# Block products of gate and up kept as running sums in PSUM, in a two-layer encoder on one core

## The chip, the cores and the metric

The kernel runs on one NeuronCore of a Trainium2 chip. The metric is the device time of one launch in microseconds (us). The kernel before was timed three times: 1349.25, 1349.61 and 1349.74 us, median 1349.61. One further execution was taken with the hardware profiler. Engines are named as in the profile: PE is TensorE, PEld its weight loads, DVE is VectorE, ACT is ScalarE, POOL is GpSimd, SP issues the DMAs.

## The reference

```python
# D_MODEL 1024, SEQ 512, FFN_HIDDEN 2816, two layers
def swiglu(x, w_gate, w_up, w_down):
    return (jax.nn.silu(x @ w_gate) * (x @ w_up)) @ w_down

for layer in range(2):
    h = attn_conv_mixer(...) if layer == 0 else retention_mixer(...)
    x = layer_norm(alpha * x + h, ln_mix_g, ln_mix_b)
    x = layer_norm(alpha * x + swiglu(x, w_gate, w_up, w_down), ln_ffn_g, ln_ffn_b)
```

Layer 0 mixes with grouped-query attention beside a depthwise convolution, layer 1 with a retention scan in two directions. Both end in the SwiGLU above, and only its two products `x @ w_gate` and `x @ w_up` (512 by 1024 by 2816 each, float32) are touched here.

## The kernel before, in words

Every float32 operand of a product is split into a high and a low part (float32r), and a product takes three matmuls: high by high, high by low, low by high (`product`, L1878 to L1882). ACT makes the high part by a copy, DVE the low part by a subtraction.

The hidden width of 2816 is 22 tiles of 128 rows (`NH`). Weights come in chunks of 1 MB, each with two hidden tiles of `w_gate` or of `w_up`: chunk `c_ffn + 2i` is the gate of pair i, `c_ffn + 2i + 1` the up of pair i. Two buffers (`raw`, `w_hi`, `w_lo`) alternate, and `load` (L408) fetches a chunk when the split of the chunk two before it in the same buffer is done. The first three chunks (`PLAIN`) are multiplied plainly. The other 19 in each layer (`FAST`) are multiplied as 2 by 2 blocks with seven block products in place of eight, in Winograd's form of Strassen's scheme. These are the block chunks. The first block chunk is the up of pair 1 (`third` in the code), the second the gate of pair 2 (`fourth`), the third the up of pair 2. The second and third are `fast_pair(2)`, pairs 3 to 9 are a loop, pair 10 is the last.

A block product (`fast_product`, L2253) is 4 steps of 3 matmuls of 128 by 128 by 256, so 12 matmuls, and a block chunk is 84. The blocks of the weights are partly sums: DVE makes three of them (`weight_sums`, L1544 to L1546), POOL a fourth in place in `raw` (`fourth_sum`, L707). ACT and DVE then split in two pieces: piece 0 is the three sums (`sum_hi`, `sum_lo`, 128x1536), piece 1 the whole chunk (`w_hi`, `w_lo`, 128x2048); `piece_hi` is L983, `piece_lo` L1550. The sums of the token side (`mix_hi`, `mix_lo`, and one block of `xT` that is replaced, `mix_split(3)` and `mix_lo_part(3)`) are made once in each layer.

PSUM has eight banks. A gate chunk uses the four of `SIDE_A`, an up chunk those of `SIDE_B`. Before the change PE writes the seven products of a block chunk in this order: a11 b11, s2 t2, s1 t1, a12 b21, s4 b22, s3 t3, a22 t4. ACT copies the first into `gate32` or `up32` (`product_copy`, L993), and PE waits for that copy ahead of the sixth product, which goes into the same bank. DVE makes the four output blocks with five additions (L1566, L1572, L1574, L1576, L1578), the last three after the chunk's last product or close to it. When both chunks of a pair are summed, ACT applies Silu to the gate (`fast_gate`, L998) and DVE multiplies it by up (`fast_up`, L1584).

What sets the order of the work is the order in which each engine's instructions are written, since every engine takes its own in that order, and semaphores between engines: `product_made`, `product_copied`, `tile_added`, `sums_made`, `piece_hi_made`, `lo_made`, `gate_made`, `h_made`. A block chunk may start on PE when its `w_lo` is made (`lo_made`) and when the additions of the chunk two before it, which used the same banks, are done (`tile_added`).

Of the kernel before, what the change touches and what calls it, by code (L numbers as in the profile page):

```python
# [98 lines left out]
ADDS = 5  # L99
# [3 lines left out]
def build_encoder(nc, ins, out):  # L103
    ctx = ExitStack()
    with ctx:
# [645 lines left out]
        def _(act):  # L751
# [204 lines left out]
            def swiglu(layer, c_ffn, c_down, pm):  # L956
# [32 lines left out]
                def product_copy(i, up, n):  # L989

                    act.wait_ge(product_made, 3 * n + 1)
# [16 lines left out]
                def fast_pair(i, last=False):  # L1008
# [3 lines left out]
                    product_copy(i, 0, n)  # L1012
                    piece_hi(up, n + 1, 1)
                    if last:
                        product_copy(i, 1, n + 1)
                        make_hi(act, Chunk(c_down))
                        rows_hi(0)
                        fast_gate(i, n)
                    else:
                        piece_hi(later, n + 2, 0)  # L1020
                        product_copy(i, 1, n + 1)
                        piece_hi(later, n + 2, 1)
                        fast_gate(i, n)
# [13 lines left out]
                act.sem_inc(hi_made, 1)  # L1037
                mix_split(3)
                piece_hi(Chunk(c_ffn + 4), fourth, 0)
                product_copy(1, 1, third)  # L1040
# [182 lines left out]
        def _(dve):  # L1223
# [300 lines left out]
            def swiglu(layer, c_ffn, c_down, pm):  # L1524
# [10 lines left out]
                def weight_sums(ch, n, first=False):  # L1535
# [3 lines left out]
                    dve.wait_ge(raw_landed[ch.s], 16 * ch.nth + 16)  # L1539
                    if first:  # L1540
                        dve.wait_ge(x_normed, 8 * (2 * layer + 1))
                    else:
                        dve.wait_ge(lo_made, ch.lo - 1)
                    mine(nc.vector.tensor_tensor(w_sum[:, 0], a21, a22, ALU.add), wait=False)  # L1544
                    mine(nc.vector.tensor_tensor(w_sum[:, 2], a11, a21, ALU.subtract))
                    nc.vector.tensor_tensor(w_sum[:, 1], w_sum[:, 0], a11, ALU.subtract).then_inc(sums_made, 1)  # L1546
# [15 lines left out]
                def first_add(up, n):  # L1562
                    dst, (a, b, c, d) = (gate32, up32)[up], BANKS_OF[up]
                    dve.wait_ge(product_made, 3 * n + 2)
                    dve.wait_ge(product_copied, n + 1)
# [954 lines left out]
```

## Time and profile before

| | |
|---|---|
| median of three runs | 1349.61 us |
| profiled execution, its own time | 1349.3 us |
| span of its instructions | 1347.5 us |
| PE busy (7880 matmuls) | 1329.9 us, 99% of the span |
| PEld busy | 1180.2 us, 88% |
| DVE busy | 970.3 us, 72% |
| ACT busy | 575.6 us, 43% |
| POOL busy | 144.5 us, 11% |
| DMA queue q1, share of 16 engines | 29.6% |

Busy time of PE is the union of its matmuls, whose ends are modelled and which overlap; how fast PE goes is read from the distance between two starts. The profiled execution's own time is 1.8 us longer than its span. The two SwiGLU stages are alike: the block chunks run from 264.04 to 455.5 us in layer 0 and 762.5 us later in layer 1.

### The profile page before, as it was taken

The numbers are of one execution on the slowest core, as the hardware profiler recorded it, in microseconds if no ns is written. First come the engines' busy times: TensorE is split into PE (matmuls) and PEld (weight loads), VectorE is DVE, ScalarE is ACT, GpSimd is POOL, SyncE is SP. The second block draws the span as 40 slices with busy tenths as digits, with TensorE's granted clock in tenths as the row PEclk, the third lists the DMA queues.
The fourth block names the chain that finished last, engine by engine and source line by source line (L and its number), as shares of the span: only waits on it lengthen the run. The fifth ranks groups of instructions, "written<-read, shape, count | busy, mean of one in ns | idle before, by whom it ended". The sixth has DMA issues, their size and how long they took to land.

```text
span 1347.5 us, 19504 instructions
## 1 busy us (share of the span) xinstructions
PE 1329.9 (99%) x7880; PEld 1180.2 (88%) x7880; DVE 970.3 (72%) x1215; ACT 575.6 (43%) x735; POOL 144.5 (11%) x141
## 2 busy tenths in 40 slices
PE   9999999999999999999999999999999999999997
PEld 8887888999999988898888888878899999998885
DVE  5999957898888533477877778763389988874336
ACT  3468834534434322345354544543154443442221
POOL 5011013111111000030000000000040111100001
PEclk9999999999999999999999999999999999999999
DMA  6210113333233323251123140324323422333321
GB/s 227 63 63 1 32 63 95 94 96 123 93 96 122 125 96 103 83 204 63 63 94 125 63 156 32 125 75 171 98 63 94 125 94 93 125 125 99 107 77 63
DMA packets 86352, 131.74 MB, mean 98 GB/s; under 512 B 2832, under 2 KB 61456, under 8 KB 86160
## 3 DMA queue, kind: packets, MB, share of 16 engines
q1 hardware_dynamic: 86288, 130.84, 29.6%
q8 instruction: 46, 0.75, 0.2%
q14 instruction: 18, 0.15, 0.0%
HBM read 126.63 MB, written 4.19 MB: 97 GB/s over the span
## 4 chain that ended last, share of the span: by engine, by line
PE 87%; DVE 8%; ACT 2%; POOL 1%; issue 1%; DMA 0%; SPq 0%; DVEq 0%; ACTq 0%
PE ps L1880 22%; PE ps L1882 21%; PE ps L1881 21%; PE ps L1958 19%; DVE acc L1264 2%; DVE w_lo L426 2%; ACT w_hi L422 1%; POOL w_lo L426 1%; PE ps L2135 1%; PE ps L1893 1%; DMA x_tok<-in_x 0%; PE ps L2322 0%; PE ps L2090 0%; PE ps L2089 0%; DVE x_tok L1504 0%
## 5 line engine op out<-in xcount | busy, mean ns | idle before, releaser
L1880 PE MATMUL ps<-xT_hi,w_hi 128*128 128x256 f32 (+1 forms) x992 | 302.2, 305 | 0.5 <-POOL w_lo L426 0.5
L1882 PE MATMUL ps<-xT_hi,w_lo 128*128 128x256 f32 (+1 forms) x992 | 301.1, 304 | 0.0
L1881 PE MATMUL ps<-xT_lo,w_hi 128*128 128x256 f32 (+1 forms) x992 | 301.1, 303 | 0.0
L426 DVE TENSOR_TENSOR w_lo<-raw,w_hi 128x2048 fp32r<-128x2048 f32 x44 | 100.9, 2292 | 185.7 <-ACT w_hi L422 185.6
L1880 PEld LDWEIGHTS ps<-xT_hi,w_hi 128*128 128x128 f32 x992 | 189.5, 191 | 8.8 <-POOL w_lo L426 1.1
L1882 PEld LDWEIGHTS ps<-xT_hi,w_lo 128*128 128x128 f32 x992 | 189.5, 191 | 7.6
L1881 PEld LDWEIGHTS ps<-xT_lo,w_hi 128*128 128x128 f32 x992 | 189.6, 191 | 7.3
L422 ACT ACTIVATE w_hi<-raw 128x2048 fp32r<-128x2048 f32 x50 | 95.7, 1915 | 210.1 <-PE ps L1958 151.7
L983 ACT ACTIVATE sum_hi<-w_sum 128x1536 fp32r<-128x1536 f32 x38 | 56.5, 1488 | 183.4 <-PE ps L1882 182.6
L1880 PE MATMUL ps<-mix_hi,sum_hi 128*128 128x256 f32 x456 | 129.0, 283 | 0.0
L1881 PE MATMUL ps<-mix_lo,sum_hi 128*128 128x256 f32 x456 | 129.0, 283 | 0.0
L1882 PE MATMUL ps<-mix_hi,sum_lo 128*128 128x256 f32 x456 | 129.0, 283 | 0.0
L1958 PE MATMUL ps<-w_hi,h_hi 128*128 128x512 f32 x352 | 109.0, 390 | 0.4 <-DVE h_lo L1588 0.4
L1958 PE MATMUL ps<-w_lo,h_hi 128*128 128x512 f32 x352 | 108.8, 389 | 0.0
L1958 PE MATMUL ps<-w_hi,h_lo 128*128 128x512 f32 x352 | 108.8, 389 | 0.0
L1550 DVE TENSOR_TENSOR w_lo<-raw,w_hi 128x2048 fp32r<-128x2048 f32 x38 | 87.1, 2292 | 17.5 <-ACT w_hi L983 17.3
L707 POOL TENSOR_TENSOR raw<-raw,w_sum 128x512 f32<-128x512 f32 x38 | 51.1, 1344 | 346.1 <-DVE w_sum L1546 346.1
L1880 PEld LDWEIGHTS ps<-mix_hi,sum_hi 128*128 128x128 f32 x456 | 87.6, 192 | 0.0
L1881 PEld LDWEIGHTS ps<-mix_lo,sum_hi 128*128 128x128 f32 x456 | 87.6, 192 | 0.0
L1882 PEld LDWEIGHTS ps<-mix_hi,sum_lo 128*128 128x128 f32 x456 | 87.6, 192 | 0.0
L1099 ACT ACTIVATE w_hi<-raw 128x1024 fp32r<-128x1024 f32 x54 | 56.0, 1055 | 72.6 <-PE ps L1882 56.4
L1958 PEld LDWEIGHTS ps<-w_hi,h_hi 128*128 128x128 f32 x352 | 65.6, 188 | 14.4 <-issue 1.1
(249 smaller groups left out, 2727.4 us busy)
## 6 DMA issues: line engine op xcount, KB each, us to landing
raw<-in_l_w_in SPq DMA_DIRECT2D x33, 1024.0 KB, 5.2
raw<-in_l_ffn_w_gate SPq DMA_DIRECT2D x22, 1024.0 KB, 5.3
raw<-in_l_ffn_w_up SPq DMA_DIRECT2D x22, 1024.0 KB, 5.2
raw<-in_l_ffn_w_down SPq DMA_DIRECT2D x22, 1024.0 KB, 4.9
raw<-in_l_w_out SPq DMA_DIRECT2D x12, 1024.0 KB, 5.1
x_tok<-in_x SPq DMA_DIRECT2D x4, 512.0 KB, 6.9
x_kept<-x_tok SPq DMA_DIRECT2D x1, 2048.0 KB, 11.6
x_tok<-x_kept SPq DMA_DIRECT2D x4, 512.0 KB, 8.1
```

What stands on the lines that cost most here:

```text
L422: act.activation(w_hi[ch.s][:], raw[ch.s][:], ACT.Copy).then_inc(hi_made, 1)
L426: eng.tensor_tensor(w_lo[ch.s][:], raw[ch.s][:], f32(w_hi[ch.s][:]), ALU.subtract)\
L707: nc.gpsimd.tensor_tensor(w[:, 0:4, P:2 * P], w[:, 4:8, 0:P], w_sum[:, 1], ALU.subtract).then_inc(fourth_made, 1)
L983: nc.scalar.activation(piece(ch, j, w_hi, sum_hi[(ch.first - c_ffn) % 2][:]), piece(ch, j, raw, w_sum[:].rearrange("p j k n -> p j (k n)") ...
L1099: nc.scalar.activation(hi, src, ACT.Copy).then_inc(ret_hi, 1)
L1264: nc.vector.scalar_tensor_tensor(acc[:, ct, :], zpad[:, ct, k:k + SEQ], conv_par[:, ct, k:k + 1], acc[:, ct, :], ALU.mult, ALU.add).then_i ...
L1550: made = nc.vector.tensor_tensor(piece(ch, j, w_lo, sum_lo[(ch.first - c_ffn) % 2][:]), piece(ch, j, raw, w_sum[:].rearrange("p j k n -> p ...
L1880: nc.tensor.matmul(dst, a[0], b[0], start=start, stop=False, skip_group_check=goes_on)
L1881: nc.tensor.matmul(dst, a[0], b[1], start=False, stop=False, skip_group_check=goes_on)
L1882: return nc.tensor.matmul(dst, a[1], b[0], start=False, stop=stop, skip_group_check=goes_on)
L1893: last = nc.tensor.transpose(ps[:, turn_bank(stage, t, half), k * P:(k + 1) * P], x_tok[:, t, (4 * half + k) * P:(4 * half + k + 1) * P], ...
L1958: last = nc.tensor.matmul(ps[:, t + 4 * half, :], sT(a, row)[:, tok], (hi, lo)[b][:, k, N * half:N * half + N], start=(row == 0 and a == b ...
```

## The change

In the block chunks PE no longer puts each product in a place of its own. Three banks of a side are used, called x, y and z. PE writes a11 b11 into x and s1 t1 into z; then it adds s2 t2 onto x, writes a12 b21 into y, adds s3 t3 onto x, s4 b22 onto z, and a22 t4 onto x. ACT copies x after its first product (`first_copy`), then z after its first and x after its second (`other_copies`), and PE waits for a copy before it adds onto what was copied: ahead of the third product for the first copy, ahead of the fifth for the third. DVE makes three additions of 256 columns (two in `outer_adds`, one in `last_add`), and PE waits for the first of them ahead of the seventh product. One output block is never copied: Silu and the final multiplication read it in PSUM. Silu becomes three instructions, the multiplication three.

The three weight sums of a chunk are no longer one piece of DVE's program: two stand ahead of `outer_adds` and the third behind it, except at the start of the stage. There the order is rewritten on ACT and DVE, as the rows below show. The numbers of matmuls and their sizes are the same.

```diff
-ADDS = 5
+ADDS = 3
+PRODUCTS = 5
+COPIES = 3
...
                 # ACT
-                def product_copy(i, up, n):
-                    act.wait_ge(product_made, 3 * n + 1)
+                def first_copy(i, up, n):
+                    act.wait_ge(product_made, PRODUCTS * n + 1)
                     act.wait_ge(h_made, h0 + 2 * i)
                     nc.scalar.activation((gate32, up32)[up][:, 0, 0:256], ps[:, BANKS_OF[up][0], 0:256], ACT.Copy)\
                         .then_inc(product_copied, 1)
+                def other_copies(up, n):
+                    act.wait_ge(product_made, PRODUCTS * n + 2)
+                    nc.scalar.activation((gate32, up32)[up][:, 1, 256:512], ps[:, BANKS_OF[up][2], 0:256], ACT.Copy)\
+                        .then_inc(product_copied, 1)
+                    act.wait_ge(product_made, PRODUCTS * n + 3)
+                    nc.scalar.activation((gate32, up32)[up][:, 0, 256:512], ps[:, BANKS_OF[up][0], 0:256], ACT.Copy)\
+                        .then_inc(product_copied, 1)
                 def fast_gate(i, n):
                     act.wait_ge(tile_added, ADDS * n + ADDS)
-                    nc.scalar.activation(gate32[:], gate32[:], ACT.Silu).then_inc(gate_made, 2)
+                    act.wait_ge(chunk_used, c_ffn + 2 * i + 1)
+                    nc.scalar.activation(gate32[:, 1, 0:256], ps[:, BANKS_OF[0][0], 0:256], ACT.Silu)
+                    nc.scalar.activation(gate32[:, 0, :], gate32[:, 0, :], ACT.Silu)
+                    nc.scalar.activation(gate32[:, 1, 256:512], gate32[:, 1, 256:512], ACT.Silu).then_inc(gate_made, 2)
...
                     piece_hi(up, n + 1, 0)
-                    product_copy(i, 0, n)
+                    first_copy(i, 0, n)
                     piece_hi(up, n + 1, 1)
+                    other_copies(0, n)
...
                 # DVE
+                def outer_adds(up, n):
+                    dst, (x, y, z, _) = (gate32, up32)[up], BANKS_OF[up]
+                    dve.wait_ge(product_made, PRODUCTS * n + 4)
+                    dve.wait_ge(product_copied, COPIES * n + 2)
+                    nc.vector.tensor_tensor(dst[:, 1, 256:512], dst[:, 1, 256:512], ps[:, x, 0:256], ALU.add).then_inc(tile_added, 1)
+                    nc.vector.tensor_tensor(dst[:, 0, 0:256], dst[:, 0, 0:256], ps[:, y, 0:256], ALU.add).then_inc(tile_added, 1)
+                def last_add(up, n):
+                    dst, (x, y, z, _) = (gate32, up32)[up], BANKS_OF[up]
+                    dve.wait_ge(product_made, PRODUCTS * n + 5)
+                    dve.wait_ge(product_copied, COPIES * n + 3)
+                    nc.vector.tensor_tensor(dst[:, 0, 256:512], dst[:, 0, 256:512], ps[:, z, 0:256], ALU.add).then_inc(tile_added, 1)
                 def fast_up(i, n):
...
                     dve.wait_ge(gate_made, h0 + 2 * i + 2)
                     dve.wait_ge(tile_added, ADDS * n + ADDS)
-                    nc.vector.tensor_tensor(h32[:, 2 * i:2 * i + 2, :] if isinstance(i, int) else h32[:, bass.ds(2 * i, 2), :], gate32[:], up32[:], ALU.mult).then_inc(h_made, 2)
+                    nc.vector.tensor_tensor(rows(0), gate32[:, 0, :], up32[:, 0, :], ALU.mult)
+                    nc.vector.tensor_tensor(rows(1)[:, 256:512], gate32[:, 1, 256:512], up32[:, 1, 256:512], ALU.mult)
+                    dve.wait_ge(chunk_used, c_ffn + 2 * i + 2)
+                    nc.vector.tensor_tensor(rows(1)[:, 0:256], gate32[:, 1, 0:256], ps[:, BANKS_OF[1][0], 0:256], ALU.mult).then_inc(h_made, 2)
...
                 # DVE, start of the stage
-                weight_sums(Chunk(c_ffn + 4), fourth)
+                for j in range(3):
+                    weight_sums(Chunk(c_ffn + 4), fourth, j)
+                piece_lo(Chunk(c_ffn + 4), fourth, 0)
                 mix_lo_part(3)
-                piece_lo(Chunk(c_ffn + 4), fourth, 0)
+                outer_adds(1, third)
                 piece_lo(Chunk(c_ffn + 4), fourth, 1)
-                first_add(1, third)
-                weight_sums(Chunk(c_ffn + 5), fourth + 1)
-                other_adds(Chunk(c_ffn + 3), 1, third)
+                last_add(1, third)
                 fast_up(1, third)
+                for j in range(3):
+                    weight_sums(Chunk(c_ffn + 5), fourth + 1, j)
                 fast_pair(2)
...
                 # PE
-                    fast_product(ps[:, b0, 0:256], a11, b11).then_inc(product_made, 1)
-                    fast_product(ps[:, b1, 0:256], s2, t2).then_inc(product_made, 1)
-                    fast_product(ps[:, b2, 256:512], s1, t1)
-                    fast_product(ps[:, b3, 0:256], a12, b21)
-                    fast_product(ps[:, b3, 256:512], s4, b22)
-                    pe.wait_ge(product_copied, n + 1)
-                    fast_product(ps[:, b0, 256:512], s3, t3).then_inc(product_made, 1)
+                    x, y, z = (ps[:, b, 0:256] for b in (b0, b1, b2))
+                    fast_product(x, a11, b11).then_inc(product_made, 1)
+                    fast_product(z, s1, t1).then_inc(product_made, 1)
+                    pe.wait_ge(product_copied, COPIES * n + 1)
+                    fast_product(x, s2, t2, start=False).then_inc(product_made, 1)
+                    fast_product(y, a12, b21)
+                    pe.wait_ge(product_copied, COPIES * n + 3)
+                    fast_product(x, s3, t3, start=False).then_inc(product_made, 1)
+                    fast_product(z, s4, b22, start=False).then_inc(product_made, 1)
                     if first and up:
                         pe.wait_ge(mix_lo_made, 4 * layer + 4)
-                    fast_product(ps[:, b2, 0:256], a22, t4).then_inc(chunk_used, 1)
+                    pe.wait_ge(tile_added, ADDS * n + 1)
+                    fast_product(x, a22, t4, start=False).then_inc(chunk_used, 1)
```

DVE's instructions at the start of the block chunks, layer 0. `up_96` is `up32`, `sum_lo_88` and `w_lo_57` are the two pieces of the second block chunk, `sum_lo_89` is piece 0 of the third; L1544 to L1546 are the weight sums of the third. Before:

```order
L1550 TENSOR_TENSOR sum_lo_88<-w_sum,sum_hi_86 128x1536 [waits piece_hi_made]
L1550 TENSOR_TENSOR w_lo_57<-raw_53,w_hi_55 128x2048 [waits piece_hi_made]
L1566 TENSOR_TENSOR up_96<-up_96,ps 128x256 [waits product_copied,product_made]
L1544 TENSOR_TENSOR w_sum<-raw_52 128x512 [waits lo_made,raw_landed0]
L1545 TENSOR_TENSOR w_sum<-raw_52 128x512
L1546 TENSOR_TENSOR w_sum<-w_sum,raw_52 128x512 [waits dve_own]
L1572 TENSOR_TENSOR up_96<-up_96,ps 128x256 [waits tile_added,product_made]
L1574 TENSOR_TENSOR up_96<-up_96,ps 128x512 [waits tile_added]
L1576 TENSOR_TENSOR up_96<-up_96,ps 128x256 [waits chunk_used]
L1578 TENSOR_TENSOR up_96<-up_96,ps 128x2x256 [waits tile_added]
L1584 TENSOR_TENSOR h_85<-gate_95,up_96 128x1024 [waits tile_added,gate_made]
L1550 TENSOR_TENSOR sum_lo_89<-w_sum,sum_hi_87 128x1536 [waits piece_hi_made]
```

And in the changed kernel, whose lines have moved (L1562 to L1566 are the weight sums, L1586 and L1587 `outer_adds`, L1593 `last_add`, L1600 to L1603 `fast_up`):

```order
L1570 TENSOR_TENSOR sum_lo_88<-w_sum,sum_hi_86 128x1536 [waits piece_hi_made]
L1580 TENSOR_TENSOR xT_lo<-x_mix_92,xT_hi 128x4x256 [waits mix_hi_made]
L1586 TENSOR_TENSOR up_96<-up_96,ps 128x256 [waits product_copied,product_made]
L1587 TENSOR_TENSOR up_96<-up_96,ps 128x256
L1570 TENSOR_TENSOR w_lo_57<-raw_53,w_hi_55 128x2048 [waits piece_hi_made]
L1593 TENSOR_TENSOR up_96<-up_96,ps 128x256 [waits product_copied,product_made]
L1600 TENSOR_TENSOR h_85<-gate_95,up_96 128x512 [waits tile_added,gate_made]
L1601 TENSOR_TENSOR h_85<-gate_95,up_96 128x256
L1603 TENSOR_TENSOR h_85<-gate_95,ps 128x256 [waits chunk_used]
L1562 TENSOR_TENSOR w_sum<-raw_52 128x512 [waits lo_made,raw_landed0]
L1564 TENSOR_TENSOR w_sum<-raw_52 128x512
L1566 TENSOR_TENSOR w_sum<-w_sum,raw_52 128x512 [waits dve_own]
```

`w_lo` of the second block chunk has moved behind the two outer additions of the first, and the weight sums of the third have moved from ahead of the first chunk's last additions to behind its multiplication, whose last instruction waits for the end of the chunk (`chunk_used`).

ACT at the same place, before (`sum_hi_86` and `w_hi_55` belong to the second block chunk, `sum_hi_87` to the third, `up_96` and `gate_95` are the copies of the first and of the second):

```order
L973 ACTIVATE xT_hi<-x_mix_92 128x4x256 [waits chunk_used,mix_made]
L983 ACTIVATE sum_hi_86<-w_sum 128x1536 [waits chunk_used,sums_made]
L993 ACTIVATE up_96<-ps 128x256 [waits h_made,product_made]
L983 ACTIVATE w_hi_55<-raw_53 128x2048 [waits fourth_made,raw_landed1]
L983 ACTIVATE sum_hi_87<-w_sum 128x1536 [waits chunk_used,sums_made]
L993 ACTIVATE gate_95<-ps 128x256 [waits h_made,product_made]
```

And now:

```order
L985 ACTIVATE sum_hi_86<-w_sum 128x1536 [waits chunk_used,sums_made]
L995 ACTIVATE up_96<-ps 128x256 [waits h_made,product_made]
L975 ACTIVATE xT_hi<-x_mix_92 128x4x256 [waits chunk_used,mix_made]
L1000 ACTIVATE up_96<-ps 128x256 [waits product_made]
L1003 ACTIVATE up_96<-ps 128x256 [waits product_made]
L985 ACTIVATE w_hi_55<-raw_53 128x2048 [waits fourth_made,raw_landed1]
L985 ACTIVATE sum_hi_87<-w_sum 128x1536 [waits chunk_used,sums_made]
L995 ACTIVATE gate_95<-ps 128x256 [waits h_made,product_made]
```

The block of `xT` has moved behind the first copy, two copies stand ahead of `w_hi_55`, and the first copy of the second block chunk (`gate_95`) still stands behind `sum_hi_87`, which waits for the third chunk's weight sums.

## Rows read from the trace of the kernel before

**Rows 1.** The page, busy time of each engine over the span.

```profile
PE 1329.9 (99%) x7880; PEld 1180.2 (88%) x7880; DVE 970.3 (72%) x1215; ACT 575.6 (43%) x735; POOL 144.5 (11%) x141
```

**Rows 2.** Waits of PE over the span: us in total, times, longest.

```profile
PE ps L2322 <- DVE y_tok L1783: 1.6, 2, 0.9
PE ps L2019 <- POOL ident L634: 1.5, 1, 1.5
```

**Rows 3.** Windows over the block chunks; busy (x) by engine, PEclk, DMA share, GB/s.

```profile
264.00:455.00 191.00, 191.00 (x1593) 190.96 (x1593) 165.55 (x193) 78.66 (x68) 23.34 (x18) 1.00 0.35 109
1026.00:1217.00 191.00, 191.00 (x1592) 190.88 (x1591) 165.56 (x193) 78.75 (x68) 23.31 (x18) 1.00 0.35 109
```

**Rows 4.** Timeline of PE, first block chunk, layer 0: start, duration (us).

```profile
264.04 0.28 PE L1880 MATMUL ps<-xT_hi,w_hi 128*128 128x256 f32 x1
...
265.35 0.28 PE L1882 MATMUL ps<-xT_hi,w_lo 128*128 128x256 f32 x1
265.47 0.28 PE L1880 MATMUL ps<-mix_hi,sum_hi 128*128 128x256 f32 x1
```

**Rows 5.** Timeline of DVE at the first block chunks, layer 0.

```profile
265.82 1.22 DVE L1560 TENSOR_TENSOR xT_lo<-x_mix,xT_hi 128x1024 fp32r<-128x1024 f32 x1 [1.44 <-ACT xT_hi L973]
267.19 1.76 DVE L1550 TENSOR_TENSOR sum_lo<-w_sum,sum_hi 128x1536 fp32r<-128x1536 f32 x1 [0.15 <-ACT sum_hi L983]
269.26 2.29 DVE L1550 TENSOR_TENSOR w_lo<-raw,w_hi 128x2048 fp32r<-128x2048 f32 x1 [0.31 <-ACT w_hi L983]
271.47 0.41 DVE L1566 TENSOR_TENSOR up<-up,ps 128x256 f32<-128x256 f32 x1
271.80 0.69 DVE L1544 TENSOR_TENSOR w_sum<-raw 128x512 f32<-128x512 f32 x1
272.40 0.69 DVE L1545 TENSOR_TENSOR w_sum<-raw 128x512 f32<-128x512 f32 x1
273.12 0.69 DVE L1546 TENSOR_TENSOR w_sum<-w_sum,raw 128x512 f32<-128x512 f32 x1
...
276.06 1.23 DVE L1584 TENSOR_TENSOR h<-gate,up 128x1024 f32<-128x1024 f32 x1
```

**Rows 6.** Timeline of ACT at the same place.

```profile
264.24 0.60 ACT L966 ACTIVATE gate<-ps 128x512 f32<-128x512 f32 x1 [4.84 <-PE ps L1882]
264.73 1.05 ACT L973 ACTIVATE xT_hi<-x_mix 128x1024 fp32r<-128x1024 f32 x1
265.68 1.48 ACT L983 ACTIVATE sum_hi<-w_sum 128x1536 fp32r<-128x1536 f32 x1
267.06 0.37 ACT L993 ACTIVATE up<-ps 128x256 f32<-128x256 f32 x1
267.32 1.91 ACT L983 ACTIVATE w_hi<-raw 128x2048 fp32r<-128x2048 f32 x1
```

**Rows 7.** Timeline of POOL and PE where PE waited in the plain chunks.

```profile
230.23 4.62 POOL L426 TENSOR_TENSOR w_lo<-raw,w_hi 128x2048 fp32r<-128x2048 f32 x1 [1.40 <-ACT w_hi L422]
...
234.45 0.28 PE L1882 MATMUL ps<-xT_hi,w_lo 128*128 128x256 f32 x1
234.90 0.39 PE L1880 MATMUL ps<-xT_hi,w_hi 128*128 128x256 f32 x1 [0.17 <-POOL w_lo L426]
235.13 0.28 PE L1881 MATMUL ps<-xT_lo,w_hi 128*128 128x256 f32 x1
```

**Rows 8.** Lines by form, ACT, 264 to 455 us: count, busy, mean ns, idle before.

```profile
L983 ACT ACTIVATE sum_hi<-w_sum 128x1536 fp32r<-128x1536 f32 x18 | 26.8, 1488 | 91.2 <-PE ps L1882 91.2
L998 ACT ACTIVATE gate<-gate 128x1024 f32<-128x1024 f32 x9 | 9.4, 1046 | 0.0
```

**Rows 9.** Timeline of POOL, fourth sum of the third block chunk.

```profile
273.90 1.30 POOL L707 TENSOR_TENSOR raw<-raw,w_sum 128x512 f32<-128x512 f32 x1 [8.15 <-DVE w_sum L1546]
```

**Rows 10.** Windows over PE's last matmuls and the end, columns as in rows 3.

```profile
1335.00:1340.00 5.00, 3.40 (x16) 2.47 (x14) 4.07 (x10) 1.24 (x2) 0.80 (x2) 1.00 0.24 91
1340.00:1347.00 7.00, 0.00 (x0) 0.00 (x0) 4.88 (x9) 0.00 (x0) 0.99 (x1) 0.71 0.31 116
```

More of the change, by code:

```diff
@@ L1020, in fast_pair @@
                         piece_hi(later, n + 2, 0)
-                        product_copy(i, 1, n + 1)
+                        first_copy(i, 1, n + 1)
                         piece_hi(later, n + 2, 1)
+                        other_copies(1, n + 1)
                         fast_gate(i, n)
@@ L1037, in swiglu @@
                 act.sem_inc(hi_made, 1)
+                piece_hi(Chunk(c_ffn + 4), fourth, 0)
+                first_copy(1, 1, third)
                 mix_split(3)
-                piece_hi(Chunk(c_ffn + 4), fourth, 0)
-                product_copy(1, 1, third)
+                other_copies(1, third)
                 piece_hi(Chunk(c_ffn + 4), fourth, 1)
@@ L1593, in fast_pair @@
                     n = fast_nth(layer, i, 0)
-                    for j in range(PIECES):
-                        piece_lo(up, n + 1, j)
-                    first_add(0, n)
+                    piece_lo(up, n + 1, 0)
+                    piece_lo(up, n + 1, 1)
                     if not last:
-                        weight_sums(later, n + 2)
-                    other_adds(gate, 0, n)
+                        weight_sums(later, n + 2, 0)
+                        weight_sums(later, n + 2, 1)
+                    outer_adds(0, n)
+                    if not last:
+                        weight_sums(later, n + 2, 2)
+                    last_add(0, n)
                     if last:
                         make_lo(dve, Chunk(c_down))
+                        outer_adds(1, n + 1)
                         rows_lo(0)
                     else:
-                        for j in range(PIECES):
-                            piece_lo(later, n + 2, j)
-                    first_add(1, n + 1)
-                    if not last:
-                        weight_sums(later_up, n + 3)
-                    other_adds(up, 1, n + 1)
+                        piece_lo(later, n + 2, 0)
+                        piece_lo(later, n + 2, 1)
+                        weight_sums(later_up, n + 3, 0)
+                        weight_sums(later_up, n + 3, 1)
+                        outer_adds(1, n + 1)
+                        weight_sums(later_up, n + 3, 2)
+                    last_add(1, n + 1)
                     fast_up(i, n + 1)
@@ L1618, in swiglu @@
                 nc.vector.tensor_tensor(x_t1, x_t1, f32(xT_lo[:, 0:4, tok0]), ALU.subtract).then_inc(mix_made, 1)
-                weight_sums(Chunk(c_ffn + 3), third, first=True)
+                for j in range(3):
+                    weight_sums(Chunk(c_ffn + 3), third, j, first=True)
                 nc.vector.tensor_tensor(x_b12, x_b22, x_b12, ALU.subtract).then_inc(mix_made, 1)
@@ L2251, in swiglu, with fast_product @@
                 feature_tiles(ch, SIDE_A[0:2], lambda m: pe.wait_ge(gate_made, NH * layer + m + 1))
-                def fast_product(dst, a, b):
+                def fast_product(dst, a, b, start=True):
                     for k in range(4):
-                        last = product(dst, tuple(x[:, k] for x in a), tuple(x[:, k] for x in b), k == 0, k == 3)
+                        last = product(dst, tuple(x[:, k] for x in a), tuple(x[:, k] for x in b), start and k == 0, k == 3, goes_on=not start)
                     return last
```

50 lines of the change are left out of this document (24 added, 26 removed).

## The prediction

> **What bounds the kernel now.** I read the page first: PE is busy for 1329.9 of 1347.5 us [rows 1]. So only two things can move the time: the number and the spacing of matmuls, and the time in which PE waits. The view of PE's waits comes next. Over the whole span its largest entry is 1.6 us in two waits, and its longest single wait is 1.5 us, at the start of the program [rows 2]; none of the rows shown lies in the block chunks. The windows over the block chunks of both layers say so outright: PE is busy for 191.00 of 191.00 us, DVE for 165.6, ACT for 78.7, at a granted clock of 1.00 [rows 3]. Busy PE alone could hide a loose spacing, so I read the starts in the timeline: 264.04, 265.35 eleven matmuls later and 265.47 for the next, hence 0.12 us each [rows 4]. A block product of 12 is 1.44 us, a block chunk of 84 is 10.08 us. PE has nothing to give back here unless a matmul itself becomes cheaper. What DVE and ACT save is worth nothing by itself; what they deliver late costs its full lateness.
>
> Weight loads are busy all the time as well: they leave 0.04 us in the first window and 0.12 us in the second [rows 3].
>
> **The change part by part.** Matmuls: seven products of 12 before and after, the same sizes, 38 block chunks in the two layers. They now add onto what is in the bank; inside each product 11 of 12 matmuls did so already, at the same 0.12 us [rows 4]. I take 0. What a spacing that changes would cost is a rival below.
>
> DVE, for a pair of chunks: five additions of 0.41, 0.41, 0.69, 0.41 and 0.69 twice and a multiplication of 1.23, in all 6.5 us, become six additions of 0.41 and a multiplication of about 0.69 + 0.41 + 0.41, in all 4.0 us (durations of 256, 512 and 1024 columns in [rows 5]). So 2.5 us less for a pair. ACT: two copies of 0.37 [rows 6] and a Silu of 1.05 [rows 8] become six copies of 0.37 and Silu in three parts (0.60 for 512 columns as in [rows 6], about 0.37 for 256), in all 3.6 against 1.8 us. ACT is busy for 78.7 of 191 us, so there is room. Neither moves PE.
>
> New waits of PE in the steady chunks. Time is counted from the first matmul of a chunk. ACT's Silu at 264.24 was released by the product that ended where the next began, at 264.04, so a product is known 0.20 us after the start of the next one [rows 4, 6]. First copy: its product is known at 1.44 + 0.20 = 1.64; ACT starts `sum_hi` at 0.20 (PE's chunk end is what it waits for [rows 8]) and has it done at 1.69, so the copy is over at about 2.0, and PE wants it at 24 x 0.12 = 2.88. Then ACT makes `w_hi`, 1.91, until about 3.8, and the copies of z and x follow; the second x is known at 4.52, copied at 4.9, wanted at 5.76. The first outer addition: product known at 7.40, added at 7.8, wanted at 8.64. DVE is free for it: `w_hi` at 3.8, `w_lo` 2.29 until 6.1, two sums until 7.3. The smallest margin is 0.8 us. Its cover is that ACT and DVE stay on this schedule; without it the cost is each chunk's lateness, 38 times. I take 0, and keep for the range a lateness of 0 to 0.15 us a chunk.
>
> What a late release costs beyond its lateness: `w_lo` of POOL ended at 230.23 + 4.62 = 234.85, PE was due at 234.57 and started at 234.90, and the matmul after it came 0.23 later and not 0.12 [rows 7]. So lateness plus 0.05 plus 0.11, about 0.16.
>
> The start of the stage, layer 0. Here the chain is not steady, and I follow it through the new order with the old durations. The first block chunk starts at 264.04 as before. Consecutive instructions of DVE start some 0.08 us before the one ahead has ended, of ACT 0.10 (0.41 from 271.47, next at 271.80; 1.48 from 265.68, next at 267.06 [rows 5, 6]).
>
> Copies: Silu ends at 264.84, then `sum_hi` 264.74 to 266.22, first copy until 266.5, wanted at 266.92. The block of xT until 267.45, copy of z until 267.8, copy of x from 268.56 to 268.94, wanted at 269.80. All in time.
>
> First stall: the outer additions wait for five products, 264.04 + 60 x 0.12 + 0.20 = 271.44. They run until 272.18. Only then comes `w_lo` of the second block chunk, whose high part has been ready since 268.84 + 1.91 = 270.75: 272.10 + 2.29 = 274.39. Before, it ran from 269.26 to 271.55 [rows 5]. PE wants it at 264.04 + 10.08 = 274.12. Late by 0.27, with the release 0.43. The second block chunk starts in effect at 274.55.
>
> Second stall: behind this `w_lo` stand the last addition (until 274.72), the multiplication in three parts (274.75 to 276.10; its last part waits for the chunk's end, known at 274.32, so it is not what holds it), and then the three sums of the third block chunk, which before started at 271.80 [rows 5]. They start at 276.02, and by the old distances (0.60, 0.72, then 0.69) end at 278.03. ACT's next instruction is `sum_hi` of that chunk, 278.06 to 279.54, and the first copy of the second block chunk stands behind it, although its product is known at 276.2: 279.44 + 0.37 = 279.81. PE wants that copy ahead of its third product, at 274.55 + 2.88 = 277.43. Late by 2.38, with the release 2.54.
>
> After that: the third product runs from 279.97 in effect. POOL makes the fourth sum in 1.30 [rows 9] until 279.4; `w_hi` 279.7 to 281.6, copies until 282.2, wanted at 282.85. `w_lo` from 281.66 to 283.95, two sums until 285.15, first outer addition 285.06 to 285.48, wanted at 285.73: in time by 0.25, the tightest place. From the third block chunk on the steady schedule holds, since DVE has gained the 2.5 us a pair. The last pair feeds the down projection: first outer addition of up at 7.8, wanted at 8.64, behind the split of the down weights, which is over by 6.2. In time.
>
> Nothing gives the delay back: later waits of PE are for DVE and ACT work that itself follows from PE. Layer 1 repeats the chunk times 762.51 us later and its windows are equal [rows 3].
>
> **The sum.** 0.43 + 2.54 = 2.97 for a layer, 5.9 for both. Bounds: if DVE carried no backlog at all, the multiplication's last part would start at 274.35, the sums at 274.7 and end at 276.7, the copy at 278.5 against 277.0 wanted, so 1.5 + 0.16 a layer, 3.3 in all; below that the written order does not let it go. Above: 0.15 x 38 = 5.7 more. The profiled execution took 1349.3, so 1355.2 for such a one; the median of the runs is 0.3 above it, so 1355.5.
>
> **The rivals.**
>
> (a) Spacing falls, faster. If the block products met DVE's traffic, 2.5 us less of it a pair might let matmuls start closer. The place is all 3192 matmuls of the block chunks, the price 3.2 us for each nanosecond, and it decides from 2.7 ns on, where 5.9 is paid back and 2.7 us more gained: at 3 ns 1349.6 + 5.9 - 9.6 = 1345.9. For it: PE is the whole of the stage. Against: the starts keep 0.12 in [rows 4], at which time DVE is idle (its next row starts at 265.82 after 1.44 us without work [rows 5]). Chance 0.03.
>
> (b) The chain is shorter than I make it, or the change does less than it says at the start, and at most half of the lower bound is paid: 1349.6 to 1352, say 1351. Against it stands the order on both engines. Chance 0.08.
>
> (c) The steady margins don't hold, and each chunk waits as well: 1355.5 + 5.7 = 1361.2. For it: three waits in a chunk where there was one, and one place at the start with 0.25 us. Against: 0.8 us in the others. Chance 0.10.
>
> (d) The clock falls in the 2.5 us stall. After PE's last matmul, at about 1338.4 (3.40 us busy from 1335), the granted clock stayed at 1.00 to 1340, and averaged 0.71 from 1340 to 1347 [rows 10], that is 1.2 GHz for 4.1 us of the 7 and 2.4 before, so it fell some 4.5 us after the last matmul. The stall is shorter than that. If it fell nevertheless and stayed low for another 4.1 us, half the matmuls of that time would be lost, 2 us a layer: 1359.6. Chance 0.05. The Trainium skill (TensorE: Matmul & The Clock Gate, Part 1: The HAM clock gate) has the clock fall after idle time and come back with activity; the row agrees that it falls, and no row shows so short a gap doing it.
>
> (e) More increments of semaphores delay PE: six a chunk where there were four, 76 more. The product that ends at 265.35 signals, and the next matmul starts 0.12 later like all others [rows 4]; 0.01, which is what the row can hide, would be 0.8 us, 1356.3. Chance 0.04. The Trainium skill (TensorE: Matmul & The Clock Gate, The cost: per-tile semaphore tail) gives 26.3 ns for an increment; as an estimate by that page 76 of them would be 2.0 us, and the sum 7.9 in place of 5.9. The trace does not agree.
>
> **How the numbers follow.** My forecast, two stalls a layer, has 0.70, with 1353.0 to 1357.5 as its own range. With (e) and part of (b) below, (d) and part of (c) above, 1352.4 to 1359.6 holds about 8 in 10 or a little more. A measurement of this kernel can tell 0.2% from no change, 2.7 us: faster is below 1346.9, slower above 1352.3. Faster: (a), and little of it, 0.03. Same: (b), 0.09. Slower: the rest, 0.88.
>
> **What would show it.** In the profile after, PE's waits have two new entries in each layer: one of some 0.3 us ahead of the second block chunk, released by DVE's `w_lo`, and one of some 2.3 us three products on, released by ACT's copy into the gate tile, with `sum_hi` right ahead of it. Everything behind is shifted by 3.0 us and then by 5.9. The window over the rest of the block chunks still has PE busy throughout. I am wrong if the first copy runs before that `sum_hi`, if PE has a wait in each chunk, or if the starts are no longer 0.12 apart.

## The result and the profile after

| | before | after |
|---|---|---|
| median of the runs, us | 1349.67 (1349.20 to 1350.21) | 1357.04 (1355.99 to 1358.36, 6 runs) |
| profiled execution, us | 1349.3 | 1357.15 |
| its span, us | 1347.5 | 1355.3 |
| ratio | | 1.0054 [1.0043, 1.0065] |

The change is slower by 7.4 us, 5.9 were forecast. The page's busy line, to be read against [rows 1], has 38 us less on DVE, 27 more on ACT, and PE busy 3.2 us longer with the same 7880 matmuls:

```profile
PE 1333.1 (98%) x7880; PEld 1182.7 (87%) x7880; DVE 932.2 (69%) x1179; ACT 603.0 (44%) x847; POOL 143.7 (11%) x141
```

The view of PE's waits (us in total, times, longest) has the two entries that the prediction named and that [rows 2] do not have:

```profile
PE ps L1907 <- ACT gate L995: 4.7, 2, 2.4
PE ps L2360 <- DVE y_tok L1810: 1.6, 2, 0.9
...
PE ps L1907 <- DVE w_lo L1570: 0.3, 2, 0.2
```

The windows, with the columns of [rows 3], split the block chunks of each layer into the first 40 us and the rest:

```profile
264.00:304.00 40.00, 37.45 (x308) 36.85 (x307) 30.33 (x35) 19.36 (x25) 5.15 (x4) 1.00 0.27 86
304.00:455.00 151.00, 151.00 (x1260) 151.00 (x1260) 115.67 (x137) 72.14 (x98) 18.10 (x14) 1.00 0.35 111
1026.00:1066.00 40.00, 37.46 (x282) 36.37 (x281) 29.77 (x36) 16.23 (x21) 5.15 (x4) 0.96 0.34 106
1066.00:1217.00 151.00, 151.00 (x1261) 151.00 (x1260) 117.99 (x139) 71.14 (x96) 18.15 (x14) 1.00 0.33 106
```

Two things are to be seen. All waits of the block chunks lie in the first 40 us; behind them PE is busy 151.00 of 151.00. And in layer 1 the granted clock is 0.96 there, where both windows of before over the block chunks have 1.00 [rows 3]. The timeline of PE around the two stalls of layer 0, and at a third, smaller one:

```profile
274.04 0.28 PE L1909 MATMUL ps<-xT_hi,w_lo 128*128 128x256 f32 x1
274.49 0.39 PE L1907 MATMUL ps<-xT_hi,w_hi 128*128 128x256 f32 x1 [0.17 <-DVE w_lo L1570]
274.71 0.28 PE L1908 MATMUL ps<-xT_lo,w_hi 128*128 128x256 f32 x1
...
277.34 0.28 PE L1909 MATMUL ps<-mix_hi,sum_lo 128*128 128x256 f32 x1
280.00 0.39 PE L1907 MATMUL ps<-mix_hi,sum_hi 128*128 128x256 f32 x1 [2.38 <-ACT gate L995]
280.22 0.28 PE L1908 MATMUL ps<-mix_lo,sum_hi 128*128 128x256 f32 x1
...
285.74 0.28 PE L1909 MATMUL ps<-xT_hi,w_lo 128*128 128x256 f32 x1
285.97 0.39 PE L1907 MATMUL ps<-xT_hi,w_hi 128*128 128x256 f32 x1
286.20 0.28 PE L1908 MATMUL ps<-xT_lo,w_hi 128*128 128x256 f32 x1
```

Starts should be 0.12 apart. What is above that is what a stall costs PE, and here and below it is counted in the interval with the wait and in the one behind it: 0.33 + 0.10 = 0.43, 2.54 + 0.10 = 2.64 and 0.11 + 0.11 = 0.22 us, 3.3 for layer 0. (The view puts only the idle part down as the wait, 2.38 of the 2.64.) ACT and DVE show why:

```profile
278.19 1.48 ACT L985 ACTIVATE sum_hi<-w_sum 128x1536 fp32r<-128x1536 f32 x1 [7.41 <-DVE w_sum L1566]
279.58 0.37 ACT L995 ACTIVATE gate<-ps 128x256 f32<-128x256 f32 x1
```

```profile
272.15 2.28 DVE L1570 TENSOR_TENSOR w_lo<-raw,w_hi 128x2048 fp32r<-128x2048 f32 x1
...
276.14 0.69 DVE L1562 TENSOR_TENSOR w_sum<-raw 128x512 f32<-128x512 f32 x1
276.75 0.69 DVE L1564 TENSOR_TENSOR w_sum<-raw 128x512 f32<-128x512 f32 x1
277.47 0.69 DVE L1566 TENSOR_TENSOR w_sum<-w_sum,raw 128x512 f32<-128x512 f32 x1
...
281.78 2.29 DVE L1570 TENSOR_TENSOR w_lo<-raw,w_hi 128x2048 fp32r<-128x2048 f32 x1 [0.32 <-ACT w_hi L985]
284.17 0.69 DVE L1562 TENSOR_TENSOR w_sum<-raw 128x512 f32<-128x512 f32 x1
284.78 0.68 DVE L1564 TENSOR_TENSOR w_sum<-raw 128x512 f32<-128x512 f32 x1
285.50 0.42 DVE L1586 TENSOR_TENSOR gate<-gate,ps 128x256 f32<-128x256 f32 x1
```

The weight sums that ended at 273.81 in [rows 5] end at 278.16, ACT idles 7.41 us for them, and the first copy of the second block chunk stands behind `sum_hi`.

Layer 1 has stalls of 0.43 and 2.63 us in the same places. Then comes what layer 0 does not have, in three windows around it (columns as above):

```profile
1040.00:1047.30 7.30, 4.76 (x37) 4.45 (x37) 5.56 (x9) 3.32 (x3) 1.27 (x1) 1.00 0.47 144
1047.30:1050.80 3.50, 3.50 (x19) 3.50 (x18) 3.13 (x3) 0.78 (x3) 0.00 (x0) 0.51 0.02 5
1050.80:1060.00 9.20, 9.20 (x79) 9.20 (x79) 5.56 (x7) 4.75 (x7) 1.29 (x1) 1.00 0.38 114
```

```profile
1049.62 0.41 PE L1909 MATMUL ps<-xT_hi,w_lo 128*128 128x256 f32 x1
1049.84 0.41 PE L1907 MATMUL ps<-mix_hi,sum_hi 128*128 128x256 f32 x1
1050.05 0.41 PE L1908 MATMUL ps<-mix_lo,sum_hi 128*128 128x256 f32 x1
```

PE resumed at 1045.79, and 1.5 us later the granted clock fell to 0.51, the 1.2 GHz level: 16 matmuls came 0.213 apart in place of 0.12, 1.5 us in all, and as PE is late by that, the third stall does not arise. Layer 1 pays 0.43 + 2.63 + 1.5 = 4.6. Together 7.9 us; the spans differ by 7.8.

### The profile page after: what moved, and what is told of

Same layout as the page of the kernel before. It is cut to its first block, busy times and chain, and to the rows that moved or that the text cites. A ratio compares the mean times of both kernels' runs of the same rounds, so it can differ in the third digit from the quotient of the medians.

```text
span 1355.3 us, 19646 instructions
## 1 busy us (share of the span) xinstructions
PE 1333.1 (98%) x7880; PEld 1182.7 (87%) x7880; DVE 932.2 (69%) x1179; ACT 603.0 (44%) x847; POOL 143.7 (11%) x141
## 4 chain that ended last, share of the span: by engine, by line
PE 81%; DVE 8%; issue 7%; ACT 2%; POOL 2%; DVEq 0%; POOLq 0%; ACTq 0%
PE ps L1907 20%; PE ps L1909 19%; PE ps L1908 19%; PE ps L1985 19%; DVE acc L1281 2%; DVE w_lo L428 2%; ACT w_hi L424 1%; POOL w_lo L428 1%; PE ps L2162 1%; PE ps L1920 1%; PE ps L2360 0%; PE ps L2046 0%; PE ps L2117 0%; PE ps L2116 0%; POOL raw L709 0%
## 5 line engine op out<-in xcount | busy, mean ns | idle before, releaser
L1570 DVE TENSOR_TENSOR sum_lo<-w_sum,sum_hi 128x1536 fp32r<-128x1536 f32 x38 | 66.8, 1758 | 46.8 <-ACT sum_hi L985 45.2
```

Of the source, the lines that this page charges most:

```text
L1570: made = nc.vector.tensor_tensor(piece(ch, j, w_lo, sum_lo[(ch.first - c_ffn) % 2][:]), piece(ch, j, raw, w_sum[:].rearrange("p j k n -> p ...
```

## The experiments

The kernel before measured 1349.4 in the same rounds. Edits are against the changed kernel unless another is named.

**The order at the start put back, running sums kept (5 rounds).** On ACT the split of the whole second block chunk (`w_hi`) stands right behind the first copy again. On DVE its `w_lo` stands ahead of the outer additions again, and the third block chunk's weight sums ahead of the last addition and the multiplication.

```diff
 # ACT
-mix_split(3)
-other_copies(1, third)
 piece_hi(Chunk(c_ffn + 4), fourth, 1)
+other_copies(1, third)
+mix_split(3)
 # DVE
+piece_lo(Chunk(c_ffn + 4), fourth, 1)
 mix_lo_part(3)
 outer_adds(1, third)
-piece_lo(Chunk(c_ffn + 4), fourth, 1)
-last_add(1, third)
-fast_up(1, third)
 for j in range(3):
     weight_sums(Chunk(c_ffn + 5), fourth + 1, j)
+last_add(1, third)
+fast_up(1, third)
```

> The changed kernel with its block products as they are; only the start of the block chunks is reordered: ACT splits the second block chunk whole right behind the first copy, DVE makes its w_lo ahead of the outer additions and the third chunk's weight sums ahead of the last addition. Theory (all of the loss is late delivery at the start of the stage, running sums cost nothing): first outer addition done at 272.1, wanted at 272.68, w_lo of the second chunk at 270.6, wanted at 274.12, its first copy at 276.2, wanted at 277.0; no wait of PE in the block chunks, 1349.7 us, ratio to before 1.000 within 0.001. Rival (adding onto what is in the bank, more semaphores or more waits cost in each chunk): some of the loss stays in all 38 chunks, 1351.5 us or more.

Measured: 1351.18 (1350.78 to 1351.85), ratio 1.0013 [1.0004, 1.0022]. Most of the loss is gone, so it sits in the order. But 1.8 us stay, where none were expected: PE still loses 0.57 us ahead of the third product of the second block chunk and 0.24 ahead of the seventh, 1.6 in two layers. ACT, DVE and POOL of this run:

```profile
277.34 0.38 ACT L995 ACTIVATE gate<-ps 128x256 f32<-128x256 f32 x1 [1.16 <-DVE h L1603]
```

```profile
275.09 1.49 DVE L1600 TENSOR_TENSOR h<-gate,up 128x512 f32<-128x512 f32 x1
276.50 0.41 DVE L1601 TENSOR_TENSOR h<-gate,up 128x256 f32<-128x256 f32 x1
276.84 0.41 DVE L1603 TENSOR_TENSOR h<-gate,ps 128x256 f32<-128x256 f32 x1
```

```profile
274.73 1.29 POOL L709 TENSOR_TENSOR raw<-raw,w_sum 128x512 f32<-128x512 f32 x1 [8.67 <-DVE w_sum L1566]
```

The copy has a second condition that the prediction did not follow: it overwrites `gate32`, so `first_copy` waits for the multiplication of the pair ahead (`h_made`). And the first part of that multiplication took 1.49 us, not 0.69; POOL's fourth sum ran beside it until 276.02. Whether that is the reason, and whether the copy would be in time without it, is tested below.

**The weight sums alone moved ahead (3 rounds).** The three `weight_sums` go ahead of `last_add` and `fast_up`; the rest stays as in the changed kernel.

> The changed kernel, but DVE makes the third block chunk's weight sums ahead of the last addition and the multiplication instead of behind them; w_lo of the second chunk stays behind the outer additions. Theory: the wait of 0.43 us ahead of the second chunk stays; the sums end at 276.5 in place of 278.2, sum_hi at 278.0, the first copy at 278.3 against 277.5 wanted, so a wait of about 1.0 us in place of 2.6; some 0.2 us ahead of the seventh product; 1.6 us a layer, 1353 us and no fall of the granted clock. Rival (the copy waits for something else, the multiplication by h_made): the wait stays above 2 us.

Measured: 1357.22 (1355.51 to 1358.42), ratio 1.0058 [1.0042, 1.0073], a miss by 4 us: nothing gained in the median. (The four runs lie far apart. In the profiled ones PE's second stall went from 2.64 to 2.30 us, and the clock fell behind it in layer 0.) `sum_hi` is done at 277.99, as expected, but:

```profile
276.50 1.49 ACT L985 ACTIVATE sum_hi<-w_sum 128x1536 fp32r<-128x1536 f32 x1 [5.81 <-DVE w_sum L1566]
279.14 0.38 ACT L995 ACTIVATE gate<-ps 128x256 f32<-128x256 f32 x1 [1.15 <-DVE h L1603]
```

```profile
276.91 1.48 DVE L1600 TENSOR_TENSOR h<-gate,up 128x512 f32<-128x512 f32 x1
...
278.64 0.41 DVE L1603 TENSOR_TENSOR h<-gate,ps 128x256 f32<-128x256 f32 x1
```

With the sums ahead, the multiplication is late instead and ends at 279.05, 1.06 us after `sum_hi`. The copy needs both. Two things make the multiplication late: it stands behind the late `w_lo` and the sums, and its first part takes 1.48 us again, 0.79 more than in the changed kernel, with POOL's sum beside it from 276.55 to 277.83. So most of the 1.06 us comes from POOL and not from the order.

**The stall filled with matmuls (5 rounds).** If the clock falls because PE is idle, 19 extra matmuls (about 2.3 us, into the fourth bank of the side, which the changed kernel does not use) must keep it up, and change nothing else.

```diff
+if first and not up:
+    for k in range(19):
+        nc.tensor.matmul(ps[:, b3, 0:256], a11[0][:, k % 4], b11[0][:, k % 4], start=(k == 0), stop=(k == 18))
 pe.wait_ge(product_copied, COPIES * n + 1)
```

> The changed kernel with 19 extra matmuls of 128x256 on PE ahead of the long wait in the second block chunk of each layer, into the fourth bank of the side, which nobody reads. 19 x 0.12 = 2.3 us, shorter than the wait of 2.4 us they stand in. Theory (the granted clock falls in some runs because PE stands idle there, and each fall costs 1.0 to 1.3 us; that is why the changed kernel's runs lie at 1356.0, 1357.0 and 1358.4): no fall, all runs within 0.4 us of 1356.0. Rival (the levels come from something else, such as DMA or the run): the spread of 2.4 us stays, or the matmuls add their time and it is 1360 us.

**The changed kernel again, on the same chip (5 rounds).**

> The changed kernel unchanged, to be compared with the filled one in the same rounds. Theory: runs at three levels, about 1356.0, 1357.1 and 1358.4 us for no, one and two layers with a fall of the granted clock; median 1357.0. Rival: one level with noise.

Measured: filled 1356.13 (1355.72 to 1356.84), ratio 1.0051 [1.0037, 1.0065]; the change itself 1357.77 (1357.10 to 1358.98), ratio 1.0065 [1.0051, 1.0079]. The windows over the first 40 us, of the filled kernel and then of the change run again:

```profile
264.00:304.00 40.00, 39.73 (x327) 39.15 (x326) 30.33 (x35) 19.36 (x25) 5.19 (x4) 1.00 0.28 85
1026.00:1066.00 40.00, 39.72 (x312) 38.48 (x311) 30.69 (x37) 17.61 (x23) 5.17 (x4) 1.00 0.34 106
```

```profile
264.00:304.00 40.00, 37.45 (x297) 37.00 (x296) 29.21 (x34) 19.46 (x25) 5.15 (x4) 0.96 0.27 86
1026.00:1066.00 40.00, 37.44 (x288) 35.97 (x287) 30.95 (x37) 16.71 (x22) 5.15 (x4) 1.00 0.34 106
```

This time the fall is in layer 0 and layer 1 is spared. With the stall filled, PE is nearly as late at its third product (2.52 us against 2.64), but the clock stays at 1.00 in both layers. The median is 1.6 us lower, about the price of one fall, and every filled run (1355.72 to 1356.84, mean granted clock 0.998 or 0.999) lies below every run of the change (1357.10 to 1358.98, 0.996 or 0.997). Two expectations failed: the filled runs do not all lie within 0.4 us of 1356.0, and the three separate levels for no, one or two falls cannot be told apart in the five times of the change (1357.10, 1357.62, 1357.77, 1358.70, 1358.98).

**The sums late in the kernel before (3 rounds).** The kernel before, with `weight_sums(Chunk(c_ffn + 5), fourth + 1)` moved from ahead of `other_adds(...)` and `fast_up(...)` to behind them.

> The kernel before with only DVE's order at the start changed: the third block chunk's weight sums behind the additions and the multiplication of the first. Theory: sums at 278.8, sum_hi at 280.3, copy at 280.6, and PE, which there wants the copy only ahead of the sixth product, at 281.3, does not wait for it; w_lo of the third chunk is late instead, 284.7 against 284.2 wanted, so one wait of about 0.6 us a layer, 1350.9 us. So the same late sums cost 0.6 us with the old products and 2.6 us with the new: the price is the earlier wait. Rival (late sums are dear by themselves): 2 us or more a layer, 1354 us.

Measured: 1350.70 (1350.44 to 1351.45), ratio 1.0009 [1.0000, 1.0019], as expected. `sum_hi` waits here as well (until 278.78) and the copy behind it runs at 280.17, later than in the changed kernel. PE never waits for that copy, since in this kernel no product adds onto the copied bank; it waits 0.63 us a layer for the third block chunk's `w_lo`. The late sums cost 2.6 us a layer only together with the new wait.

**Waits of 1 and of 2 us in each pair (1 round each).** To see from what length on a wait costs more than itself: the order put back as in the first experiment, and in the loop of pairs the first copy moved behind `w_hi`; for the longer one also two ACT copies that write banks not in use.

```diff
 piece_hi(up, n + 1, 0)
-first_copy(i, 0, n)
+# second kernel only:
+for k in (5, 7):
+    nc.scalar.activation(ps[:, k, :], w_sum[:, 0].rearrange("p k n -> p (k n)"), ACT.Copy)
 piece_hi(up, n + 1, 1)
+first_copy(i, 0, n)
```

> The reordered kernel, with ACT's first copy of the gate chunk behind the split of the whole chunk (w_hi) in the loop of pairs 3 to 9: 14 waits of PE in the two layers. Theory: copy done at 3.8 us after the chunk's start, wanted at 2.88: 0.9 late, with the release 1.06 us each, 14.8 us in all, 1364.5 us; the granted clock does not fall at waits of this length. Rival (it falls at short waits too): slow stretches of matmuls behind some of the 14.

> As the kernel with waits of 1 us, with two more ACT copies of 512 columns ahead of w_hi: copy done at 4.8 us, wanted at 2.88, 1.9 late, 2.06 us each, 28.8 us in all, plus the clock. Theory (a wait of about 2 us lets the clock fall by chance, as in one of two layers of the changed kernel): the granted clock falls behind some of the 14 waits but not behind all, each fall costing 1.0 to 1.5 us; 1378 us and up to 20 us more. Rival (the fall in the changed kernel had to do with that place in the program): none of the 14 falls.

Measured: 1365.34 (ratio 1.0118) and 1396.55 (ratio 1.035, two runs of 1398.38 and 1394.71, the first of them profiled). The first kernel has 14 stalls of 0.93 + 0.10 = 1.03 us, 14.4 in all; on top of 1351.2 that is 1365.6, so they cost themselves and no more. The second has 14 of 1.97 + 0.10 = 2.07, 29.0 in all, which makes 1380.2; the profiled run lies 18.2 above that. Windows over the loop in the kernel with short waits, then in the one with long ones:

```profile
290.00:440.00 150.00, 144.61 (x1193) 143.19 (x1192) 114.92 (x136) 68.16 (x94) 18.07 (x14) 1.00 0.30 98
```

```profile
290.00:460.00 170.00, 157.34 (x1212) 155.91 (x1210) 116.92 (x138) 75.92 (x109) 18.07 (x14) 0.93 0.27 88
1080.00:1216.00 136.00, 125.14 (x970) 123.93 (x969) 93.23 (x113) 59.53 (x83) 15.49 (x12) 0.94 0.28 93
1216.00:1240.00 24.00, 22.19 (x185) 21.99 (x184) 17.55 (x20) 12.42 (x18) 2.58 (x2) 1.00 0.27 87
```

PE's timeline has a stretch of 15 matmuls at 0.21 us behind 12 of the 14 long waits; a pair with one takes 23.7 us, one without 22.2. 12 x 1.5 = 18.0, the missing 18.2. The 14 waits are alike, so their length alone does not decide. In layer 0 the slow matmuls begin 0.3 us after PE has resumed at the first wait and later at each following one, 1.4 us at the seventh. In layer 1 they go from 0.7 to 1.4 us over five waits, and the two waits behind those are the spared ones.

**POOL's fourth sum held back (3 rounds).** The first experiment's kernel, in which the pair 2 fourth sum waits until the multiplication is over.

```diff
 # POOL
-with pool.Fori(2, NH // 2) as i:
+fourth_sum(2, 0)
+pool.wait_ge(h_made, NH * layer + 4)
+fourth_sum(2, 1)
+with pool.Fori(3, NH // 2) as i:
```

> The reordered kernel, with one wait added on POOL: its fourth sum for the third block chunk starts only when the multiplication of the first pair is done. In the reordered kernel that POOL instruction ran from 274.73 to 276.03, and DVE's multiplication of 512 columns (all operands in SBUF) beside it took 1.49 us, where it took 0.69 in the changed kernel with POOL idle. Theory (the two slow each other down): the multiplication takes 0.7 us, the first copy of the second chunk is done 0.8 us sooner and PE's wait of 0.57 us for it goes to 0.0 or 0.1; the fourth sum and w_hi are later by 1.7 us, so PE waits ahead of the fifth product instead, 0.4 to 0.6 us: about the same time, 1351.0. Rival (the multiplication is slow for its own reason, such as writing h32): it still takes 1.5 us.

Measured: 1354.46 (1354.37 to 1355.33), ratio 1.0037 [1.0024, 1.0050]. The mechanism that was expected for the multiplication shows; the time is a miss of 3.5 us. DVE and then POOL of this run:

```profile
274.93 0.69 DVE L1603 TENSOR_TENSOR h<-gate,up 128x512 f32<-128x512 f32 x1
275.54 0.42 DVE L1604 TENSOR_TENSOR h<-gate,up 128x256 f32<-128x256 f32 x1
275.87 0.41 DVE L1606 TENSOR_TENSOR h<-gate,ps 128x256 f32<-128x256 f32 x1
276.20 1.75 DVE L1573 TENSOR_TENSOR sum_lo<-w_sum,sum_hi 128x1536 fp32r<-128x1536 f32 x1
```

```profile
276.37 2.74 POOL L709 TENSOR_TENSOR raw<-raw,w_sum 128x512 f32<-128x512 f32 x1 [10.45 <-DVE h L1606]
```

The multiplication is back at 0.69 and PE no longer waits for the first copy: in this order `h_made` holds PE up only through the slow multiplication. But POOL's sum now meets `sum_lo` and takes 2.74 us where it took 1.30 [rows 9]. `w_hi` needs it, the copies of z and x stand behind `w_hi`, and PE loses 1.78 us ahead of the fifth product and 0.76 ahead of the seventh: 5.1 in two layers.

**The remaining waits taken away (5 rounds).** The first experiment's kernel with a semaphore of its own for the second block chunk's first copy, raised once the 512 columns are multiplied that it overwrites. In pair 2 the outer additions stand ahead of the second weight sum.

```diff
 # ACT, first_copy and other_copies
-act.wait_ge(h_made, h0 + 2 * i)
+if isinstance(i, int) and i == 2 and up == 0:
+    act.wait_ge(gate_free, layer + 1)
+else:
+    act.wait_ge(h_made, h0 + 2 * i)
...
+if isinstance(i, int) and i == 2:
+    act.wait_ge(h_made, h0 + 4)
 # DVE, fast_up
+if isinstance(i, int) and i == 1:
+    first_rows.then_inc(gate_free, 1)
 # DVE, fast_pair
-weight_sums(later, n + 2, 1)
+if not (isinstance(i, int) and i == 2):
+    weight_sums(later, n + 2, 1)
 outer_adds(0, n)
+if isinstance(i, int) and i == 2:
+    weight_sums(later, n + 2, 1)
```

> The reordered kernel, with the last two waits of PE in the block chunks taken away: the first copy of the second block chunk waits only for the first 512 columns of the multiplication (those it overwrites), and in the second chunk the outer additions stand ahead of the second weight sum. Theory: the copy is done 0.33 us before PE wants it, the outer addition 0.6 us before, no wait of PE is left in the 38 block chunks, and the kernel with all its running sums in PSUM takes what the kernel before takes, 1349.5 us, ratio within 0.0007 of 1. Rival (running sums cost something in each chunk): 1350.5 us or more with no wait shown. It can't be faster than before, since PE had no wait in the block chunks there.

Measured: 1349.47 (1349.31 to 1349.94, 11 runs) against 1349.41, ratio 1.0000 [0.9991, 1.0009]. The copy now runs 0.9 us earlier than in the first experiment (0.65 when counted from ACT's first instruction in the stage), although the multiplication still takes 1.49, and PE has no wait left in the block chunks. The windows can be laid on [rows 3]:

```profile
276.44 0.39 ACT L999 ACTIVATE gate<-ps 128x256 f32<-128x256 f32 x1 [0.50 <-DVE h L1606]
```

```profile
264.00:455.00 191.00, 191.00 (x1593) 190.96 (x1592) 148.86 (x175) 92.35 (x124) 23.27 (x18) 1.00 0.35 110
1026.00:1217.00 191.00, 191.00 (x1591) 190.88 (x1590) 149.04 (x175) 92.36 (x124) 23.32 (x18) 1.00 0.34 109
```

DVE has 16.6 us less work in each window, ACT 13.7 more, PE is full as before. The running sums by themselves cost nothing and gain nothing. No version beats the kernel before: this one ties with it.

## Why the prediction was right, and where it was not

*What bounds the kernel.* Right. The last experiment has less DVE work, more ACT work and the same time.

*First stall, 0.43 a layer.* Right: 0.43 in both, released by `w_lo` at 274.43, which was worked out as 274.39.

*Second stall, 2.54.* Right in place, chain and size: 2.64 and 2.63. The chain ran 0.13 us late, the three sums ended at 278.16 and not at 278.03, and PE at its third product was itself some 0.03 late.

*The reasoning behind it was incomplete.* The late `sum_hi` was taken for the only thing that holds the copy. The wait for `h_made` stands in the rows of the order ahead of the prediction, and was passed over. In the changed kernel that costs nothing: the multiplication ended at 276.22 and `sum_hi` at 279.67. It shows as soon as the sums are early, where the copy waits for the multiplication until 279.05. The prediction also has no term for DVE and POOL beside each other, which is 0.79 us of that delay and the whole of the 0.57 us in the first experiment. Its floor of 1.5 + 0.16 us a layer was meant for the order as written; the first experiment, with 0.81, has another.

*"In time by 0.25, the tightest place."* Wrong: it was late by 0.06. The first outer addition ran from 285.50, not 285.06, to 285.92; PE, itself 0.13 late, wanted it at 285.86, and with the release it lost 0.22 in layer 0. `w_lo` was 0.12 later than worked out, and both edges that wait on a semaphore came with no overlap: the sum behind `w_lo` started 0.10 after its end, the addition 0.04 after the sum, where 0.08 ahead of the end had been reckoned. The same distances, 0.72 against 0.60, were already in [rows 5].

*The clock, rival (d).* This is the step that failed: "it fell some 4.5 us after the last matmul. The stall is shorter than that." The profile has the fall behind one of its two long stalls, 1.5 us, and the run again has it behind one too. The windows at the program's end were read as a length that a gap must have, but they show only when the clock fell there. Of the gap between 7.8 and 5.9 it is 1.5; the rest is 2 x 0.10 and 0.22. That 1357.04 still lies in the forecast's own range, up to 1357.5, is in part luck: the clock's price was not in the sum, and the same kernel measured again gave 1357.77. The Trainium skill (TensorE: Matmul & The Clock Gate, Part 1: The HAM clock gate) has the clock fall after idle time and return with activity; the traces agree. The experiment with filled stalls, whose clock stays at 1.00 and whose runs all lie below those of the change, shows that idle time of PE is the cause.

*Rivals (a), (c) and (e).* The last experiment has every running sum, every copy and every increment in each of the 38 block chunks and measures 1.0000: spacing did not fall, steady margins hold, and the increments cost nothing that shows, 0 +- 1.2 us by the interval. By the estimate from the Trainium skill (TensorE: Matmul & The Clock Gate, The cost: per-tile semaphore tail) they would be 2.0 us. That section gives its figure for a tail behind tiles that each signal; for one signal in 12 matmuls or more the measurement decides against it. *(b)* did not come about.

Not tried: a changed order in which the copy stands ahead of the late `sum_hi` while the weight sums stay late.

## What to carry to other kernels

When an engine's result becomes a condition of the bounding engine, list every semaphore it waits for, and work out each one's time: curing the latest exposes the next, here only 0.3 us earlier. A wait of the bounding engine can have a price of its own behind it, the clock. At the start of a stage the steady margins do not hold, and there each place with less than half a microsecond of margin is a loss to be reckoned with. Work taken off an engine that delivers in time anyway was worth nothing here: 16.6 us less on DVE in each window, and the same time.

## What the runs showed of the hardware

**The clock can fall behind waits of 2 us.** Behind stalls of 2.3 to 2.6 us (2.04 to 2.38 of it idle) at an otherwise full PE the granted clock went from 1.00 to about 0.5, the 1.2 GHz level, in three of six: one of two each in the change, the change again and the sums early. Behind those of 2.07 us (1.81 idle) it fell in 12 of 14. Behind those of 1.03 us it fell in none of 14, and behind those of 1.78 us (1.52 idle, POOL held back) in neither of two. The fall began 0.3 to 1.5 us after PE had resumed, on matmuls that had nothing to do with the wait, and cost 1.5 us. Why some waits are spared is open; equal waits in one kernel are treated differently, so it is not their length alone.

**DVE and POOL slow each other down.** DVE's multiplication of 512 columns takes 0.69 us alone and 1.49 beside POOL's sum that began first (0.93 us of overlap, 0.80 longer); POOL's sum takes 1.30 alone and 2.74 beside DVE's `sum_lo` that began first (1.59 of overlap, 1.44 longer). So the one that comes later stands for most of the time that both share; all of these have their operands in SBUF. An addition of DVE that reads PSUM was not slowed: in the kernel before, one of 512 columns at 324.37 took its usual 0.69 us beside POOL's sum (324.09, 1.30 us). In the changed kernel's steady pairs a slow multiplication is the rule, as its lines by form from 304 to 455 us show (busy, mean ns, idle before), so the multiplication was costed too low there, with no effect on PE:

```profile
L1600 DVE TENSOR_TENSOR h<-gate,up 128x512 f32 x7 | 9.0, 1286 | 1.5 <-DVE up L1593 1.5
```

The Trainium skill (GPSIMD Engine Reference, 1. Specifications) says that the two share SBUF interfaces, with contention when DVE reads two operands from SBUF; the traces agree, by 0.80 and 1.44 us.
